# A mixture-of-experts gather with the token rows as TensorE's stationary operand

## The reference, cut to what matters

```python
probs = softmax(xt @ w_router)                  # 256 tokens, 16 experts
idx = two best experts of the best group of 4   # per token
combine = weights of the two, normalised
for e in range(16):
    h = silu(xt @ w_gate[e]) * (xt @ w_up[e])   # each matrix 1024 x 1024, fp32
    y = y + combine[:, e:e+1] * (h @ w_down[e])
h = layer_norm(ALPHA * h + y)
```

## Time and profile before

| what | value |
|---|---|
| median of 3 runs | 781.57 us (780.5 to 782.05) |
| profiled execution | 780.76 us, span 778.7 us |
| PE, weight loads | busy 740.8 us (95%), 450.5 us (58%) |
| DVE, ACT, POOL | busy 335.4, 253.5, 29.0 us |
| HBM read | 249.92 MB, 322 GB/s over the span |
| granted TensorE clock, mean | 0.991 |

### The profile page before, as it was taken

The page is one execution under the profiler, slowest core; times in us unless marked ns, Lnnn a source line. Parts: engine busy times, 40 slices in busy tenths (PEclk is TensorE's granted clock), DMA queues, the critical chain, the costliest instruction groups (busy, mean ns, idle before and its releaser), DMA issues.

```text
span 778.7 us, 12250 instructions
## 1 busy us (share of the span) xinstructions
PE 740.8 (95%) x4334; PEld 450.5 (58%) x4335; DVE 335.4 (43%) x783; ACT 253.5 (33%) x537; POOL 29.0 (4%) x59
## 2 busy tenths in 40 slices
PE   6999999999999999999999999999999898898894
PEld 5978789998889999743333333333333332333341
DVE  6687566545768777574212221222212212202205
ACT  5675535546767555421111101111111101111111
POOL 3032000000001000000000000000000000000000
PEclk9999999999999999999999999999999999999998
DMA  9795313335040866999999999999999999999994
GB/s 278 310 348 216 144 74 138 137 157 217 2 187 30 324 274 239 390 367 385 425 426 425 425 425 431 428 423 429 429 423 431 428 423 431 429 421 433 426 421 167
DMA packets 38530, 251.41 MB, mean 323 GB/s; under 512 B 6129, under 2 KB 13394, under 8 KB 24162
## 3 DMA queue, kind: packets, MB, share of 16 engines
q1 hardware_dynamic: 38352, 250.94, 78.9%
q10 hardware_dynamic: 146, 0.04, 0.0%
HBM read 249.92 MB, written 1.05 MB: 322 GB/s over the span
## 4 chain that ended last, share of the span: by engine, by line
PE 72%; SPq 14%; DMA 6%; DVE 4%; issue 1%; ACT 1%; ACTq 0%; DVEq 0%
PE ps L2194 28%; PE ps L1798 8%; PE ps L1800 8%; PE ps L1799 8%; DMA gate_x<-in_w_gate_e_dram 6%; SPq L583 3%; PE ps L2144 3%; SPq L602 2%; SPq L572 2%; PE ps L1875 2%; PE ps L2151 2%; PE ps L2132 2%; SPq L586 2%; DVE xc L1204 1%; DVE wlo L1190 1%
## 5 line engine op out<-in xcount | busy, mean ns | idle before, releaser
L2194 PE MATMUL ps<-raw,xg 128*64 128x512 f32 x512 | 117.0, 607 | 9.0 <-DMA raw<-in_w_gate_e_dram 5.9
L1798 PE MATMUL ps<-hi_h,whi 128*128 128x272 f32 (+1 forms) x384 | 111.6, 291 | 0.4 <-DVE wlo L1121 0.3
L1800 PE MATMUL ps<-hi_h,wlo 128*128 128x272 f32 (+1 forms) x384 | 109.3, 285 | 0.0
L1799 PE MATMUL ps<-lo_h,whi 128*128 128x272 f32 (+1 forms) x384 | 109.0, 284 | 0.0
L1121 DVE TENSOR_TENSOR wlo<-raw,whi 128x512 fp32r<-128x512 f32 x128 | 82.6, 687 | 38.6 <-ACT whi L751 38.0
L2194 PEld LDWEIGHTS ps<-raw,xg 128*64 128x64 f32 x512 | 38.0, 140 | 85.2 <-issue 75.8
L751 ACT CAST whi<-raw 128x512 fp32r<-128x512 f32 (+1 forms) x128 | 74.1, 619 | 14.6 <-PE ps L1800 12.3
L1798 PEld LDWEIGHTS ps<-hi_h,whi 128*128 128x128 f32 x384 | 72.3, 188 | 4.3 <-issue 2.5
L1800 PEld LDWEIGHTS ps<-hi_h,wlo 128*128 128x128 f32 x384 | 72.4, 188 | 0.0
L1799 PEld LDWEIGHTS ps<-lo_h,whi 128*128 128x128 f32 x384 | 72.3, 188 | 0.0
L2194 PE MATMUL ps<-gate_x,xg 128*64 128x512 f32 x256 | 57.1, 594 | 7.7 <-DMA gate_x<-in_w_gate_e_dram 7.7
(11 more groups left out here) (367 smaller groups left out, 1152.6 us busy)
## 6 DMA issues: line engine op xcount, KB each, us to landing
raw<-in_w_up_e_dram SPq DMA_DIRECT2D x16, 2048.0 KB, 34.1
gate_x<-in_w_gate_e_dram SPq DMA_DIRECT2D x16, 2048.0 KB, 37.1
raw<-in_w_down_e_dram SPq DMA_DIRECT2D x16, 2048.0 KB, 34.3
raw<-in_w_gate_e_dram SPq DMA_DIRECT2D x15, 2048.0 KB, 36.4
raw<-in_w_in_dram SPq DMA_DIRECT2D x28, 1024.0 KB, 9.1
down_x<-in_w_down_e_dram SPq DMA_DIRECT2D x8, 2048.0 KB, 38.0
up_x_right<-in_w_up_e_dram SPq DMA_DIRECT2D x16, 1024.0 KB, 38.8
up_x_left<-in_w_up_e_dram SPq DMA_DIRECT2D x8, 2048.0 KB, 37.7
```

The source lines that it names most:

```text
L1798: mm(o, w1, hi[:, k, c0:c0 + n], start=(k == 0), stop=False)
L1799: mm(o, w1, lo[:, k, c0:c0 + n], start=False, stop=False)
L1800: last = mm(o, w2, hi[:, k, c0:c0 + n], start=False, stop=(k == KB - 1))
L2194: last = mm(ps[r0:r0 + SLOTS, bank_no, :], lhs[:, k % 4, k // 4, :], w[:, k % 2, 512 * c:512 * c + 512], start=(k == 0), stop=(k == KB - 1))
```

## The change

`gather()` exchanges the operands. Every fourth row channel of `h1` (128 columns, 16 bytes apart) is stationary, and the 64 columns of `pick` move. The output has channels on partitions, which is the layout that `take_gathered` reads, so the copy to `xsb` and its four transposes go, in the first gather and in each unit. There are now 2 x 4 x 2 = 16 matmuls of 64 columns where there were 4 of 512.

```diff
 def gather(first=False):
-    for t in range(TT):
-        if first:
-            pe.wait_ge(s.pick_ready, t + 1)
-        for c in range(2):
-            r0 = SLOTS * c
-            last = mm(ps[r0:r0 + SLOTS, B_GATH, :], pick[:, t, 0:SLOTS], h1[:, t, 512 * c:512 * c + 512],
-                      start=(t == 0), stop=(t == TT - 1))
-    last.then_inc(s.gath_done, 1)
+    for c in range(2):
+        bank_no = B_GATE if first and c == 0 else B_XT
+        if first and c == 0:
+            pe.wait_ge(s.pick_ready, TT)
+        for a in range(4):
+            c0 = 2 * SLOTS * a + SLOTS * c
+            for t in range(TT):
+                last = mm(ps[:, bank_no, c0:c0 + SLOTS], every_fourth(h1[:, t, 512 * c:512 * c + 512], a),
+                          pick[:, t, 0:SLOTS], start=(t == 0), stop=(t == TT - 1))
+        if first or c:
+            last.then_inc(s.xt_done, 1)
...
 gather(True)
-keep_warm(0, 2)
-pe.wait_ge(s.xsb_ready, 1)
-turn_rows(B_XT, xsb[:], s.xt_done)
 pe.wait_ge(s.units_ready, 1)
...
-keep_warm(0, 2)
...
 turn_rows(B_HT, hs[:], s.ht_done)
-pe.wait_ge(s.xsb_ready, u + 2)
-turn_rows(B_XT, xsb[:], s.xt_done)
```

ACT loses both copies. The first gather uses two banks, so that DVE can take its first half while PE makes the second, and `weights_of_tokens` (the sum, the reciprocal and the product that make `comb`) moves from behind `pick` to between these halves:

```diff
-        def take_gathered(n):
-            turned_x = ps[:, B_XT, :].rearrange("p (a c s) -> p a c s", c=2, s=SLOTS)
+        def take_gathered(n, banks=(B_XT, B_XT)):
             for c in range(2):
+                if banks[0] != B_XT:
+                    dve.wait_ge(s.xt_done, c + 1)
+                    if c:
+                        weights_of_tokens()
+                turned_x = ps[:, banks[c], :].rearrange("p (a c s) -> p a c s", c=2, s=SLOTS)
```

More of the change, by code:

```diff
@@ L242, in build @@
     diag = at("diag", [P, D], F + 24576)
-    xsb = at("xsb", [P, 512], F + 2048)
     logit_parts = at("logit_parts", [P, T], F + 2048)
@@ L389, in build @@
     s.pick_ready = nc.alloc_semaphore("pick_ready")
-    s.gath_done = nc.alloc_semaphore("gath_done")
     s.xg_ready = nc.alloc_semaphore("xg_ready")
@@ L394, in build @@
     s.down_used = nc.alloc_semaphore("down_used")
-    s.xsb_ready = nc.alloc_semaphore("xsb_ready")
     s.xt_done = nc.alloc_semaphore("xt_done")
@@ L422, in build @@
     HEAD_GROUPS = 25
-    B_GATE, B_UP, B_Z, B_GATH, B_HT, B_XT, B_ACC = 0, 1, 2, 3, 0, 3, (4, 5, 6, 7)
+    B_GATE, B_UP, B_Z, B_HT, B_XT, B_ACC = 0, 1, 2, 0, 3, (4, 5, 6, 7)
     block = ctx.enter_context(nc.Block())
@@ L1029, in _ @@
                            scale=rstd[:, t:t + 1]).then_inc(s.h1_ready, 1)
-        act.wait_ge(s.gath_done, 1)
-        act.copy(xsb[:], ps[:, B_GATH, :]).then_inc(s.xsb_ready, 1)
         act.wait_ge(s.units_ready, 1)
@@ L1037, in _ @@
             act.activation(hs[:], ps[:, B_GATE, :], ACT.Sigmoid).then_inc(s.gsig_ready, 1)
-            act.wait_ge(s.gath_done, u + 2)
-            act.copy(xsb[:], ps[:, B_GATH, :]).then_inc(s.xsb_ready, 1)
             act.wait_ge(s.ht_done, u + 1)
@@ L1576, in by_slot, with weights_of_tokens @@
             return v[:, c, :].unsqueeze(2).to_broadcast([P, 4, SLOTS])
-        def take_gathered(n):
-            turned_x = ps[:, B_XT, :].rearrange("p (a c s) -> p a c s", c=2, s=SLOTS)
-            for c in range(2):
+        def weights_of_tokens():
+            own(dve.tensor_reduce(rt[:, 15, 24:24 + TT], val(9), AX.X, ALU.add))
+            own.settle()
+            own(dve.reciprocal(rt[:, 15, 28:28 + TT], rt[:, 15, 24:24 + TT]))
+            own.settle()
+            own(dve.tensor_tensor(comb[:], val(9), rt[:, 15, 28:28 + TT].unsqueeze(2).to_broadcast([P, TT, NE]), ALU.mult))
+            own.settle()
+        def take_gathered(n, banks=(B_XT, B_XT)):
+            for c in range(2):
+                if banks[0] != B_XT:
[3 more added lines that the diff above has]
+                turned_x = ps[:, banks[c], :].rearrange("p (a c s) -> p a c s", c=2, s=SLOTS)
                 dve.tensor_tensor(xg[:, :, c, :], turned_x[:, :, c, :], by_slot(gain4, c), ALU.mult).then_inc(s.xg_scaled, 1)
@@ L1644, in _ @@
         pick_tokens(0, 0)
[L1645 to L1649, removed]
         own(dve.tensor_scalar(nblk_f[:], counts[:], float(SLOTS), 1.0, ALU.is_gt, ALU.add))
@@ L1670, in _ @@
         dve.tensor_copy(blocks[:, 1, :], ends_f[:, 1 - src, 32:]).then_inc(s.units_ready, 1)
-        dve.wait_ge(s.xt_done, 1)
         dve.wait_ge(s.gain4_in, 32)
-        take_gathered(1)
+        take_gathered(1, (B_GATE, B_XT))
         dve.wait_ge(s.pick_ready, TT)
@@ L1726, in _ @@
             dve.tensor_tensor(hs[:], ps[:, B_UP, :], hs[:], ALU.mult).then_inc(s.hs_ready, 1)
-            dve.wait_ge(s.xt_done, u + 2)
+            dve.wait_ge(s.xt_done, u + 3)
             take_gathered(u + 2)
```

## The result

The changed kernel takes 890.71 us (median of 4 runs, 889.85 to 891.35) against 781.04 us for the one before: ratio 1.141, 95% interval 1.139 to 1.142. It is 109.7 us slower, where 10.5 were forecast. The profiled execution has a span of 889.0 us.

A forecast was written before the change was run, and what follows sets the result against it. Before, transfers set the end, with PE near its limit at 25.02 us a unit; after, PE bounds. Last down product: 736.8 + 0.5 + 15 x 2.18 = 770.0 against 759.52, 10.5 us later, so 792.1 us; range 785 to 801.

The forecast's parts named there:

- the 1.5 us to spare in a unit: Expert stage before: PE has 22.7 us to spare over 15 units; beyond 1.5 us a unit PE bounds to the end.
- the transposes that give nothing back: In each unit, removing the `xsb` transposes saves nothing, since PE then waits those 0.5 us for ACT's copy of `hid`.
- PE as the bound to the end: Expert stage after: PE sets a pace of 27.2 us a unit to the end, with no waits for transfers.
- 32 pairs bound by their loads: New gather: 16 fp32 matmuls are 32 pairs, paced by 128-column weight loads; 3.90 us, 2.18 us more than before.
- The pitch of a pair: New gather: time per weight load and matmul, taken as 0.122 us; each 0.01 us moves the end by 5.4 us.
- the outer bound: New gather: pair pitch of 0.18 us if striding cost these loads more than it costs a transpose's.
- Rival E: Low streaming in each unit's gather drops PE's clock to 0.50: 16 x 1.7 = 27 us more, about 819; chance 3%.
- The head's part: First unit: gate product starts 0.74 us earlier, but second gather delays the up product; net 0.5 us later.
- Rival A: Gather: striding costs nothing, pitch 0.11, gather 3.52 us; +4.4, 786.0 us; chance 16%.
- B: Gather: loads partly hidden, pitch 0.054 to 0.10, transfers stay the bound; about 782.5 us; chance 4%.
- C: Gather: pairs at the streaming pace of 0.054, whole stage about 1.5 us earlier; 780.0 us; chance 4%.
- D: Gather: loads not overlapped or striding dearer, pitch 0.164 to 0.18; +34 to +42, 815 to 824 us; chance 8%.

## Why the prediction was wrong

The direction and the structure were right: what bounds before, the 1.5 us to spare in a unit, the transposes that give nothing back, PE as the bound to the end, 32 pairs bound by their loads. Two steps failed.

**The pitch of a pair, the step that decided.** The prediction took "0.122, near the strided row, since it has the same columns, the same stride and the same traffic around it", and 0.18 as the outer bound "if striding cost these loads more than it costs a transpose's". Measured: 0.239. The error lies in the comparison. The load of a transpose is another kind than that of an fp32 matmul: contiguous ones, also of 128 columns, last 0.14 us against the 0.19 of the earlier trace rows (timeline of the kernel before):

```profile
328.50 0.91 PEld L2058 LDWEIGHTS ps<-ident,h 128*128 128x128 f32 x8
```

(0.91 less seven pitches of 0.11). I compared a strided transpose's load, 0.21 us, with a contiguous matmul's, 0.19, and so saw 0.02 where the transpose's own load had grown by 0.07, from 0.14 to 0.21. I took its pitch of 0.12 as the price of a strided load; the outer bound of 0.18 had no row behind it. The matmul's load grew by twice as much, from 0.19 to 0.33, and its pitch at a step of 16 bytes is about twice the transpose's, 0.239. The runs show that a matmul's load pays for each 16-byte stretch; why a transpose's load pays half of that for the same 128 stretches stays open. With 0.239 in the forecast's own slope of 5.4 us for each 0.01, (0.239 - 0.122) x 544 = 64 us. That is the largest term of the miss.

**The clock.** The sum put it at nothing. Rival E had the mechanism and nearly the price, 1.7 us a unit against 1.89 measured (2.04 less 0.15 that the up product loses behind any such gather), and I gave it 3%. Against it I held a stretch of 2 us in the head at half occupancy. That row could say little: in the trace after, the clock is still at 1.00 from 423 to 425 us, up to 2.6 us into the gather. I also took E as an alternative to a longer gather. At the forecast's pitch E would have been wrong in the units: with neighbouring columns, at 0.116, the clock stayed up there. In the changed kernel the pitch was twice as long, so the array streamed for half as much of the time as I had thought, and there it fell in each unit: the first error brought the second. The term is 15 x 2.04 = 31 us in the units.

The head's part follows from both. Up to the first down product it is 12.2 us instead of the 0.5 of the forecast: each of its two gathers is 3.8 us longer than forecast, and two products are slowed by about 2 each. 56 for the pitch in the units, 31 for the clock, 12 for the head and 1 for the later start of the stage are the 100 us between 110 and 10.5.

**What held.** With the pitch measured for neighbouring columns, 0.116, the forecast's sum gives 0.1 + 15 x (3.71 - 1.72) - 22.7 = 7.3, and 9.5 with the 0.15 us that each up product loses behind such a gather, a term that was missing. Measured: 791.07 - 781.35 = 9.7. Rival A, which was this kernel at 0.11, was 5 us low. Rivals B and C fall: nothing hid the loads. D was nearest in the pitch, at 0.18, and its 824 us are 67 short.

## What to carry to other kernels

Before operands are exchanged, count what each side reads in 16-byte stretches: in an fp32 matmul a step of 16 bytes doubled the read on the stationary side (0.116 to 0.239 us for 128 columns) and on the moving side (0.43 to 0.90 us for 512), while on the stationary side a step of 8 was nearly free. Take the price from a row of the same kind of instruction: a transpose's load did not show what a matmul's would cost. A layout change belongs where nobody waits: four strided transposes were hidden behind a copy, 32 strided loads were not. And where small matmuls stand behind long loads, look at the granted clock of what follows, since the product behind the gather paid for it.

## What the runs showed of the hardware that I had not expected

- The pitch of an fp32 matmul's load depends on the 16-byte stretches that it touches: with 64, 96 and 128 of them it was 0.122, 0.182 and 0.239 us, 1.9 ns each; with 32 it was 0.116. The loads of transposes touch 128 of them at a pitch of 0.12.
- The strided gather took 7.66 us whether the clock was at 1.00 throughout (128 columns moving) or at 0.50 in its second half (the changed kernel); the contiguous one took 3.71 at 1.00 and 5.7 with most of it at 0.50.
- Twice the moving columns under the same loads made the kernel 32 us faster (890.71 to 858.59): extra streaming that costs no time kept the clock up. That kernel lacks the transposes and the `keep_warm` matmuls too, so their removal alone did not lower the clock.
